# Hybrid conv/pooling encoder layer on 8 cores: the blocks of w_o and w_pgate loaded in pairs during stage 2 of the first half, where all sixteen were loaded at its beginning

## What is computed

```python
h = _rmsnorm(x, g_pre)
xa, ba, ca, za, xb, zb, ga, gb = split(h @ w_in)          # 8 x 1024 columns
ya = ((ba * conv3(ca * xa)) * silu(za)) @ w_a_out         # branch A
yb = (mixed * silu(zb)) @ w_b_out                         # branch B: pooled xb through w_grp
m  = sigmoid(ga) * ya + sigmoid(gb) * yb
o  = m @ w_o
x1 = x + _rmsnorm(o, g_post)
out = x1 + (p @ w_ple) * sigmoid(x1 @ w_pgate)
```

## Time and profile before

| | |
|---|---|
| median of 3 runs | 759.61 us (759.2 to 760.65) |
| the profiled execution | 759.77 us |
| its span, first to last instruction, slowest core | 758.2 us (cores 756.5 to 758.2) |
| TensorE busy | 745.3 us, 98% of the span |
| granted TensorE clock | 0.998 to 1.000 on every core |
| VectorE, ScalarE, GpSimd busy | 51%, 34%, 45% |
| DMA queue of GpSimd | 50.41 MB, 45.1% of the 16 DMA engines' span |
| the chain that ended last | TensorE 93%, DMA 4% |

### The profile page before, as it was taken

How to read it: one execution, slowest core, us unless ns; L and a number is a source line. 1 busy time by engine, 2 the same in 40 slices (tenths; PEclk the granted TensorE clock), 3 DMA queues, 4 the chain that set the end, 5 groups by cost and what they waited for, 6 DMA issues and landing times.

```text
span 758.2 us, 13217 instructions; the slowest of 8 cores (756.5 to 758.2 us)
## 1 busy us (share of the span) xinstructions
PE 745.3 (98%) x4386; PEld 376.5 (50%) x4386; DVE 384.3 (51%) x639; ACT 254.3 (34%) x514; POOL 339.8 (45%) x514
## 2 busy tenths in 40 slices
PE   6899999999999999999999999999999999999998
PEld 5665454444444444454545545455455555555444
DVE  4775667776622112455557666575751212224655
ACT  3533444442211111333333333343421111115453
POOL 5333555558642433342435536466582342211544
PEclk9999999999999999999999999999999999999999
DMA  8999769858995564827547384474747354306643
GB/s 184 219 149 195 92 156 167 155 109 130 172 156 78 75 92 61 139 76 138 87 85 129 78 135 79 90 132 63 152 84 119 56 80 63 55 0 202 157 119 125
DMA packets 65907, 87.82 MB, mean 116 GB/s; under 512 B 30897, under 2 KB 34737, under 8 KB 65842
## 3 DMA queue, kind: packets, MB, share of 16 engines
q0 software_dynamic: 29792, 50.41, 45.1%
q1 hardware_dynamic: 36050, 36.57, 17.4%
HBM read 117.35 MB, written 11.36 MB: 170 GB/s over the span
## 4 chain that ended last, share of the span: by engine, by line
PE 93%; DMA 4%; POOL 1%; DVE 1%; issue 1%; ACT 0%; SPq 0%; DVEq 0%; ACTq 0%; POOLq 0%
PE ps L604 74%; PE ps L829 8%; PE ps L876 7%; DMA w<-w_in 2%; PE ps L882 2%; DMA wo<-x 2%; PE ps L745 1%; PE ps L575 0%; PE ps L781 0%; POOL sp L713 0%; POOL mT L595 0%; DVE hb L562 0%; DVE sg L894 0%; ACT hb L555 0%; DVE qT L897 0%
## 5 line engine op out<-in xcount | busy, mean ns | idle before, releaser
L604 PE MATMUL ps<-hB,w 128*128 128x512 bf16 (+1 forms) x912 | 156.5, 326 | 0.0
L604 PE MATMUL ps<-hA,w 128*128 128x512 bf16 (+1 forms) x816 | 143.6, 329 | 2.6 <-DVE hA L579 1.9
L604 PEld LDWEIGHTS ps<-hB,w 128*128 128x128 bf16 x912 | 77.1, 98 | 72.0
L604 PE MATMUL ps<-hB,hA 128*128 128x512 bf16 (+1 forms) x624 | 108.6, 326 | 0.0
L604 PEld LDWEIGHTS ps<-hA,w 128*128 128x128 bf16 x816 | 69.2, 98 | 69.0 <-issue 3.7
L808 DVE SCALAR_TENSOR_TENSOR tA<-tA,ps 128x512 f32<-128x512 f32 (+1 forms) x40 | 24.3, 609 | 141.5 <-PE ps L604 141.5
L604 PE MATMUL ps<-hA,mT 128*128 128x512 bf16 x400 | 91.4, 379 | 0.0
L811 POOL TENSOR_TENSOR mT<-tA,tB 128x512 bf16<-128x512 f32 (+1 forms) x40 | 44.0, 1109 | 84.4 <-DVE tB L808 84.0
L604 PEld LDWEIGHTS ps<-hB,hA 128*128 128x128 bf16 x624 | 52.8, 98 | 49.1
L805 ACT ACTIVATE tA<-ps 128x512 f32<-128x512 f32 (+1 forms) x40 | 21.3, 533 | 152.3 <-PE ps L604 147.5
L876 PE MATMUL ps<-wpg,x1T 128*128 128x512 bf16 (+2 forms) x296 | 61.7, 362 | 0.0
(11 more groups left out here) (131 smaller groups left out, 903.0 us busy)
## 6 DMA issues: line engine op xcount, KB each, us to landing
w<-w_in POOLq DMA_DIRECT2D x75, 256.0 KB, 7.3
hA<-w_in POOLq DMA_DIRECT2D x26, 256.0 KB, 8.0
hA<-x SPq DMA_DIRECT2D x10, 512.0 KB, 3.5
y<-hA SPq DMA_DIRECT2D x10, 512.0 KB, 3.8
mT<-w_in POOLq DMA_DIRECT2D x19, 256.0 KB, 8.7
wo<-x SPq DMA_DIRECT2D x9, 512.0 KB, 8.2
wpg<-x SPq DMA_DIRECT2D x8, 512.0 KB, 13.9
w<-w_b_out POOLq DMA_DIRECT2D x14, 256.0 KB, 5.5
```

The costliest lines, as they stand in the source:

```text
L604: ins_ = e.matmul(bk.ap[:, parts[0]:parts[1]], lhsT=w.ap[:, kk, :], rhs=act(kk), start=(kk == 0), stop=(kk == 7))
```

## The change

The pair of blocks of each j is now made to wait, beside the norms, for the last matmul group of the unit (j-1, 0), that is, of the first token block of the column block before it. The pair of j = 0 has no such predecessor and waits for the norms alone, as before. Nothing else is edited.

```diff
         norm_done = list(norm_ops)
+        p2_done = []
         rl = []
...
             for name, dst, src, kk in rl[2 * j:2 * j + 2]:
                 OP('pool', lambda e, d, dst=dst, src=src, kk=kk: d(e.dma_start(out=dst[:, kk, :], in_=src[kk * 128:(kk + 1) * 128, :])), 0.57, kj - 5.0,
-                   outs=[res(f"{name}{kk}")], dma=0.524, sem=f"ld_{name}{kk}", after=norm_done, tag=f'{name}{kk}')
+                   outs=[res(f"{name}{kk}")], dma=0.524, sem=f"ld_{name}{kk}", after=norm_done + p2_done[-1:], tag=f'{name}{kk}')
...
             for k in H1.blocks:
                 p2_unit(j, k, wins[(0, 2, j)], kj + k.b * 4 * 8 * MM, all_p1 if j == 0 else ())
+            p2_done.append(H1.blocks[0].p2v[-1])
```

## The result

Changed kernel: 764.47 us, median of six runs (763.53 to 765.32). Kernel before, beside it: 759.95; one of its six runs, 816.67, was a slow one that the ratio leaves out, and the other five have a median of 759.61. The ratio is 1.006, interval 1.005 to 1.0071: **0.6% slower**, outside the predicted range. The profiled execution took 765.32 us.

The account below looks back on a forecast made before the run. TensorE was taken as the bound, busy 629.26 of 630 us from 50 to 680 us on core 2. Profiled 759.77 less 0.3, all other terms 0, gave 759.5, as a median of runs 759.3; range 758.4 to 762.0.

Parts of the forecast that it names:

- the rival of more gain: TensorE's waits before 680 us: all cores lose 0.74 us, giving 758.9, with the end untouched; chance 0.05.
- the part on stage 3: Last pair (wpg, j = 7) issues 21 us before stage 2 ends, and stage 3 comes after: no cost.
- the third load of the pairs' queue: Stage 2, w_a_out behind a pair: lands 8.5 us after the pair's first issue, 1.7 us ahead of use; cost 0.
- the upper bound: Stage 2, w_a_out behind a pair: landing 10.7 us after first issue, from the burst at 338.07; 0.5 us too late.
- added up the queue: Stage 2, j = 2, with w_ple: eleven blocks' worth through w_a_out land by 223.5, needed at about 227.2; room 3.7 us.
- the rival: Late loads before vT and qT groups of units (j, 0), j = 1 to 7: 0.5 us each, 762.8; chance 0.13.
- The wait of 0.74 us for w_in: Stage 2, second column block, core 2, 213.6 to 214.3 us: the late load's wait goes, core 2 from 758.2 to 757.4.
- The new order on TensorE: Start of stage 2: first qT group at about 201.3 rather than 206.49, its inputs ready by then; cost 0.
- the median landing of w_a_out: Stage 2, sign of being right: w_a_out lands 5.5 to 7 us after issue, w_b_out 6 to 7.
- The queue kept up: Stage 2: six blocks per column block use 0.90 of the DMA, or 10 of 13.8 us, so backlog clears before the next pair.
- a gain of 0.3 us from the lost wait: Whole kernel: slowest core goes from 758.2 to 757.9, a gain of 0.3 us and not 0.74.

Follow-up runs that it names:

- g3: Changed kernel with the final addition of tile 15 moved from GpSimd to VectorE: 760.9 us, ratio 1.0017.
- e3: Changed kernel with each pair waiting for the first matmul group of unit (j-1, 0) instead of its last, 5.2 us earlier: 762.95 us, ratio 1.0043.
- f4: Changed kernel with pairs waiting for the unit's first matmul group and tile 15's final addition moved from GpSimd to VectorE: 759.54 us, ratio 0.9996.
- h1: Changed kernel with eight extra late 64 KB loads on GpSimd, one ahead of each of tiles 8 to 15: 763.76 us.
- f3: Kernel before with four more 64 KB loads on GpSimd between 511 and 577 us, each reading a pT tile again: 759.18 us.
- g1: Kernel before with seven extra 64 KB loads on GpSimd (one early, two in stage 2, four between 348 and 444 us): 759.54 us.
- h4: Kernel before with the final addition of tile 15 moved from GpSimd to VectorE: ratio 1.0.
- e1: Kernel before with seven more satisfied wait instructions on GpSimd, in front of mT additions: 759.55 us, ratio 1.0001.
- e4: Kernel before with fourteen more satisfied wait instructions on GpSimd, in front of mT additions: 759.18 us.
- f1: Kernel before with each wo and wpg load bringing only 256 of 1024 columns, VectorE setting the rest to zero: 763.1 us.
- f2: Kernel before with the 512 KB w_ple load moved ahead of the sixteen wo and wpg blocks, nothing gated: 761.1 us.
- h2: Changed kernel with sixteen extra late 64 KB loads on GpSimd, two per tile: 761.39 us.
- h3: Kernel before with sixteen extra late 64 KB loads on GpSimd, two per tile: 760.44 us.
- e2: Changed kernel's order on all engines, but the wo and wpg loads don't wait for TensorE: 763.1 us, ratio 1.0049.
- g4: Changed kernel with only the eight wpg loads held back, the wo loads going out at the start of stage 2: 763.1 us, ratio 1.0055.
- g2: Changed kernel with seven extra 64 KB loads on GpSimd (one early, two in stage 2, four between 348 and 444 us): 764.51 us.

## Why the prediction was wrong

**The step that failed** is in the rival of more gain and in the end of the part on stage 3: "the end isn't touched", "No cost". I read the end of the trace for what computes and stores, and took what closes the program as fixed. The kernel before had a DRAIN of 4.97 us there, hidden with 1.5 us to spare (it ended at 756.5, and SyncE's, behind the last store's landing, at 758.0). The changed kernel's ends 5.7 us after VectorE's. What shows is 3.3 to 3.6 us, by the runs with tile 15's addition moved. No row of the kernel before, as far as I can see, tells that another order of the same loads would lengthen it; but its length and its slack stood in the trace, and I named neither.

**The second term, mis-sized**: the third load of the pairs' queue. I took 8.5 us from the pair's first issue to its landing, 1.7 us of margin, cost 0. In the later column blocks it was mostly so: on core 2 the pair at 244.02 and w_a_out at 246.35, landed 5.1 us later, 7.4 in all (but core 4 needed 10.1 at j = 5). In the first ones it wasn't. Core 0 needed 9.9 us at j = 1 (204.07; 206.39 + 7.6) and 10.4 at j = 2, close to the 10.7 that I had as the upper bound. The room was smaller than my 10.2 us, too: on core 2 the pair went out 0.7 us after the unit's end (244.02 for 243.31), where I had taken 0.1, and the vT group came at 253.67, so 9.65 us. For j = 2 I had added up the queue at 1.66 us for a block: w_a_out landed 20.5 us after the end of unit (0, 0). On core 0 it was 24.8 us (204.07 to 228.85): 9.9 up to the first w_a_out, and then 1.86 us for each of eight blocks' worth. The load of w_ple, 512 KB, has to wait until w_b_out has landed; GpSimd stood still 3.63 us for that and issued it at 216.42, only 2 us ahead of the pair. The waits are 0.3 to 0.7 us, one to three on a core and on four of the eight cores (on six in g3), not seven alike as the rival had it. The cost is 1.3 to 1.6 us by the runs, since the slowest core pays. The rival had the mechanism; the forecast gave it 0.13. The forecast's 759.3 plus the two terms is 763.9 to 764.5, for 764.47 measured.

On this the Trainium skill, DMA: Bandwidth & Descriptors, section "Two DMAs through the same engine are not ordered", bears with its rule that descriptors start in order within one queue of a DMA engine; the trace agrees, since issuing the pair some 5 us sooner (e3) took every one of these waits away, on all eight cores.

**What was right.** The wait of 0.74 us for w_in vanished, as did those of the other cores near 214 us; the loads issued at 188.31 and 195.36 on core 2 landed in 3.8 and 3.7 us, where the earlier trace rows have 16.4 and 17.1. The new order on TensorE cost nothing: the first qT group started without a wait (200.14 on core 2, which began about 1.2 us earlier in this execution, for the 201.3 foreseen). From 233 to 290 us the median landing of w_a_out on core 2 was 5.3 us and that of w_b_out 6.3 (for 5.5 to 7, and 6 to 7):

```profile
w<-w_a_out POOLq DMA_DIRECT2D x5, 256.0 KB, 5.3
w<-w_b_out POOLq DMA_DIRECT2D x5, 256.0 KB, 6.3
```

The queue kept up: on core 2 nothing moved in it from 243 to 245 us. And a gain of 0.3 us from the lost wait is too small to be measured: with both losses repaired (f4) the ratio is 0.9996.

**What stays open.** Why the order at 170 to 290 us sets a DRAIN at 750 us. Shown is: not the waits, not their number, not the bytes of the moved loads, not w_ple's place; late loads add 0.02 (h1) to 0.081 us (f3) each, and at some point between eight and sixteen of them the changed kernel's falls to the 6.28 us that the kernel before has with the same sixteen. A recurring clean-up of GpSimd's own records of its loads would give such a drop, but by itself it explains neither h1's 0.17 us for eight loads nor g1's 1.31 for seven. The Trainium skill says in DMA: Bandwidth & Descriptors, section "SWDGE vs HWDGE vs iDMA", that GpSimd writes its loads' descriptors by software into rings that the DMA engines work off; that the DRAIN tidies these rings is my reading, and no run here shows it. Nor did I find, in the traces, where within the run the clean-up takes place.

## What to carry to other kernels

An engine that has been idle for a while at the end can still hold the program open: read what each engine's closing instruction takes, and how far it is behind the last store, before writing "the end isn't touched". Where GpSimd issues loads and its DRAIN ends last, give it its last work some us before the others finish; here two addition instructions moved to VectorE bought back 3.3 us, and nothing where the DRAIN was hidden already (h4). And a prefetch that is spread out between urgent loads should go out so early that it is through before the next urgent load is issued. An empty queue at its issue is no sign of that. In the changed kernel the pair of j = 4 met an empty queue (core 2, windows as in the earlier trace rows, the last but one column is the DMA engines' busy share):

```profile
243.00:244.00 1.00, 1.00 (x7) 0.43 (x5) 0.35 (x1) 0.00 (x0) 0.00 (x0) 1.00 0.00 0
```

In e3 it met a working one, but was through when w_a_out was issued at 246.95, and that load landed in 3.8 us:

```profile
239.00:240.00 1.00, 1.00 (x7) 0.41 (x6) 0.00 (x0) 0.35 (x1) 1.00 (x1) 1.00 0.73 127
...
247.00:248.00 1.00, 0.95 (x6) 0.42 (x5) 0.00 (x0) 0.43 (x1) 0.52 (x1) 1.00 0.05 12
```

## What the runs showed of the hardware

GpSimd's DRAIN at the end of the program goes on for 3.7 to 9.3 us after its last addition in these kernels, where VectorE's record is 0.30 us and TensorE's 1.30. It is the same on all eight cores to within some 0.02 us. Its values, as recorded: 4.97 (before, e1, e4, f1, f2), 5.30 (f3), 6.28 (g1, h2, h3), 10.36 (changed, e2, e3, g4), 10.53 (h1), 10.61 (g2); with tile 15's addition on VectorE 5.60 for 4.97 (h4) and 10.99 for 10.36 (f4, g3), with the same time after the last addition. Three kernels of different orders and 213 or 222 loads meet at 6.28. TensorE's granted clock was 1.00 up to its last matmuls in the changed kernel (core 2, 750 to 752 us) and 0.50 from 756 us on, its last matmul being over before 754.
